# First attention of a fused block: the softmax weights scaled inside their transpose by a diagonal from VectorE, in place of a scaling on GpSimd

## What is computed

```python
# NSA half: 8 heads, two branches each that matter here (selected, window)
p = masked_softmax(q @ k.T * scale + bias, mask)      # [256 queries, 256 keys], causal
out = gate_c * o_c + gate_s * (p_s @ v_s) + gate_w * (p_w @ v_w)
# DSA half: 8 heads over a latent, keys chosen by an index score (top 64 of 256)
p = masked_softmax(q_lat @ c.T * scale + bias, chosen & causal)
o_lat = p @ c ;  o = o_lat @ w_uv
y = concatenate([out, o]) @ ev_w_out
```

## Time and profile before

| | |
|---|---|
| median of 3 runs | 1220.17 us (1218.13 to 1221.36) |
| the profiled execution | 1217.92 us, its span 1216.1 us |
| busy in the span | PE 1123.6 (92%), DVE 784.4 (64%), ACT 609.4 (50%), POOL 64.8 (5%) |
| chain that ended last | PE 75%, DVE 14%, ACT 6% |
| L1073, the scalings on POOL | 48 of them, 38.0 us busy, 805 ns mean |
| TensorE's granted clock, mean | 0.976 |

### The profile page before, as it was taken

How to read it: one execution, slowest core, us unless ns; L and a number is a source line. 1 busy time by engine, 2 the same in 40 slices (tenths; PEclk the granted TensorE clock), 3 DMA queues, 4 the chain that set the end, 5 groups by cost and what they waited for, 6 DMA issues and landing times.

```text
span 1216.1 us, 20615 instructions
## 1 busy us (share of the span) xinstructions
PE 1123.6 (92%) x8503; PEld 1004.0 (83%) x8503; DVE 784.4 (64%) x1288; ACT 609.4 (50%) x1097; POOL 64.8 (5%) x85
## 2 busy tenths in 40 slices
PE   1788999999999989989999999999789998999997
PEld 1766966889899889878899988998677887999996
DVE  7666684789898685557855446666766556444443
ACT  0341376554435356565454554546673436544543
POOL 0011086000000000000000000020000000000000
PEclk9999899999999999999999999989878999999999
DMA  8678712489999545423775653160000043655540
GB/s 369 260 291 316 270 47 70 137 297 361 361 340 347 198 150 181 173 75 130 281 259 189 227 174 107 70 237 6 1 2 20 2 153 113 211 200 176 200 144 35
DMA packets 33277, 218.31 MB, mean 180 GB/s; under 512 B 4496, under 2 KB 5264, under 8 KB 8480
## 3 DMA queue, kind: packets, MB, share of 16 engines
q1 hardware_dynamic: 33184, 217.00, 49.2%
HBM read 215.93 MB, written 1.05 MB: 178 GB/s over the span
## 4 chain that ended last, share of the span: by engine, by line
PE 75%; DVE 14%; ACT 6%; DMA 2%; issue 1%; POOL 0%; SPq 0%; DVEq 0%; ACTq 0%
PE bank L505 20%; PE bank L507 20%; PE bank L506 20%; DVE ada_acc L574 2%; PE bank L530 2%; DVE low L499 1%; DMA ring<-ada_halves 1%; DVE act_low L1450 1%; PE bank L2300 1%; PE bank L587 1%; PE bank L2302 1%; ACT high L493 1%; PE bank L1081 1%; PE bank L2288 1%; DVE y_tmp L1495 1%
## 5 line engine op out<-in xcount | busy, mean ns | idle before, releaser
L499 DVE TENSOR_TENSOR low<-ring,high 128x2048 fp32r<-128x2048 f32 (+1 forms) x139 | 317.8, 2288 | 256.2 <-ACT high L493 255.9
L493 ACT ACTIVATE high<-ring 128x2048 fp32r<-128x2048 f32 (+1 forms) x139 | 264.6, 1906 | 258.3 <-PE bank L507 199.3
L505 PE MATMUL bank<-act_high,high 128*128 128x256 f32 (+1 forms) x1112 | 321.1, 289 | 6.0 <-DVE act_low L1450 6.0
L507 PE MATMUL bank<-act_high,low 128*128 128x256 f32 (+1 forms) x1112 | 316.0, 284 | 0.0
L506 PE MATMUL bank<-act_low,high 128*128 128x256 f32 (+1 forms) x1112 | 315.7, 284 | 0.0
L505 PE MATMUL bank<-high,act_high 128*128 128x512 f32 (+1 forms) x632 | 233.8, 370 | 3.8 <-DVE act_low L2828 1.8
L506 PE MATMUL bank<-low,act_high 128*128 128x512 f32 (+1 forms) x632 | 231.4, 366 | 0.0
L507 PE MATMUL bank<-high,act_low 128*128 128x512 f32 (+1 forms) x632 | 231.3, 366 | 0.0
L505 PEld LDWEIGHTS bank<-act_high,high 128*128 128x128 f32 x1112 | 213.5, 192 | 11.2 <-DVE act_low L1450 6.8
L506 PEld LDWEIGHTS bank<-act_low,high 128*128 128x128 f32 x1112 | 213.5, 192 | 2.7 <-issue 1.7
L507 PEld LDWEIGHTS bank<-act_high,low 128*128 128x128 f32 x1112 | 213.3, 192 | 0.0
(11 more groups left out here) (479 smaller groups left out, 1325.6 us busy)
## 6 DMA issues: line engine op xcount, KB each, us to landing
ring<-chunks SPq DMA_DIRECT2D x138, 1024.0 KB, 5.0
ring<-ada_halves SPq DMA_DIRECT2D x48, 1024.0 KB, 5.6
ring<-raw_cmp SPq DMA_DIRECT2D x4, 1024.0 KB, 7.0
gate_rows<-ada_b SPq DMA_DIRECT2D x4, 512.0 KB, 6.6
bias<-bias_by_distance SPq DMA_DIRECT2D x1, 2048.0 KB, 11.8
ln_rows<-ln_g SPq DMA_DIRECT2D x4, 512.0 KB, 4.5
ln_rows<-ln_b SPq DMA_DIRECT2D x4, 512.0 KB, 6.0
hT<-xT SPq DMA_DIRECT2D x1, 1024.0 KB, 8.5
```

The source lines that it names most:

```text
L493: e.activation(weights(c)[0], in_ring(("w", c)), ACT.Copy).then_inc(*act.up("high", c))
L499: e.tensor_tensor(low, in_ring(("w", c)), high.bitcast(F32), ALU.subtract).then_inc(*vec.up("low", c))
L505: e.matmul(out_, ah, bh, start=start, stop=False)
L507: return e.matmul(out_, al, bh, start=False, stop=stop)
```

## The change

A row scaling commutes with the turn: the transpose of diag(c) z is z transposed times diag(c). The change drops step 5. In its place DVE writes, behind the coefficients of a unit, two 128x128 diagonals (the identity times the coefficients, one scalar per row; in the NSA half times the gate in the same instruction, so that the separate gate product L1329 goes). PE's turn multiplies `z` with the diagonals where it was multiplied with the identity; the shapes stay. The diagonals have three slots, at the place of a tile that the indexer is done with, and a slot is free when turn(u-3) is done, for which DVE now waits. POOL keeps `mask_bias` alone. No transfer is added, removed or moved.

```diff
@@ -389,6 +389,7 @@
         relu = mem.take("relu", 2, UC, at=ln_at + 2 * UC)
+        diag = mem.take("diag", 3, 2 * P, at=ln_at + 2 * UC)
@@ -1066,12 +1067,27 @@
-        def unit_scale_gpsimd(e, u):
-            z, st = z_of(u), st_of(u)
-            e.wait_ge(*vec.at("coef", u))
-            for t, c in PARTS:
-                x = e.tensor_scalar(z[:, c], z[:, c], st[:, 4 + t:5 + t], None, ALU.mult)
-                x.then_inc(*(pool.up("p", u) if t else pool.up()))
+        def unit_scale_vector(e, u, gate):
+
+            st = st_of(u)
+            if u >= 3:
+                e.wait_ge(*pe.at("turn", u - 3))
+            for t in range(QT):
+                c_, d_ = st[:, 4 + t:5 + t], diag[:, u % 3, tok(t)]
+                if gate is None:
+                    x = e.tensor_scalar(d_, ident, c_, None, ALU.mult)
+                else:
+                    x = e.tensor_scalar(d_, ident, c_, gate(t), ALU.mult, ALU.mult)
+                x.then_inc(*(vec.up("p", u) if t else vec.up()))
+
+        def scaled_turn_tensor(e, u):
+
+            z = z_of(u)
+            b = ps.take(e, ("turn", u), act, "pT", u)
+            e.wait_ge(*vec.at("p", u))
+            for i in range(3):
+                m = e.matmul(b[:, tok(i)], z[:, tok(i)], diag[:, u % 3, tok(min(i, 1))], start=True, stop=True)
+            m.then_inc(*pe.up("turn", u))
...
@@ -1183,7 +1199,7 @@
-                    unit_turn_tensor(e, 2 * d - 3, pool)
+                    scaled_turn_tensor(e, 2 * d - 3)
...
@@ -1320,14 +1336,13 @@
                 e.wait_ge(*act.at("e", u))
+                e.reciprocal(st[:, 4:6], st[:, 2:4]).then_inc(*vec.up("coef", u))
+                e.wait_ge(*vec.at("coef", u))
                 if u >= DSA0:
-                    e.reciprocal(st[:, 4:6], st[:, 2:4]).then_inc(*vec.up("coef", u))
-                    return
-                h, branch = NSA[u]
-                e.reciprocal(st[:, 4:6], st[:, 2:4]).then_inc(*vec.up("sums", u))
-                e.wait_ge(*vec.at("sums", u))
-                e.tensor_tensor(st[:, 4:6], st[:, 4:6], gates[:, :, 3 * h + 1 + branch], ALU.mult).then_inc(
-                    *vec.up("coef", u))
+                    unit_scale_vector(e, u, None)
+                else:
+                    h, branch = NSA[u]
+                    unit_scale_vector(e, u, lambda t: gates[:, t, 3 * h + 1 + branch:3 * h + 2 + branch])
@@ -1395,16 +1410,11 @@
-            for u in range(DSA0 + 8):
-                if u == 14:
-                    e.wait_ge(*vec.at("mask"))
-                    mask_bias(0)
-                    mask_bias(1)
-                h = u - DSA0 + 2
-                if 2 <= h < 8:
+            e.wait_ge(*vec.at("mask"))
+            for h in range(8):
+                if h >= 2:
                     e.wait_ge(*vec.at("z", DSA0 + h - 2))
-                    mask_bias(h)
-                unit_scale_gpsimd(e, u)
+                mask_bias(h)
```

More of the change, by code:

```diff
@@ L1208, in attention_tensor @@
                 if d >= 1:
-                    unit_turn_tensor(e, 2 * d - 2, pool)
+                    scaled_turn_tensor(e, 2 * d - 2)
             e.wait_ge(*act.at("ql", 7))
             sparse_logits_tensor(e, 0)
-            unit_turn_tensor(e, 13, pool)
+            scaled_turn_tensor(e, 13)
             sparse_logits_tensor(e, 1)
@@ L1218, in attention_tensor @@
             for r in range(2):
-                unit_turn_tensor(e, 14 + r, pool)
+                scaled_turn_tensor(e, 14 + r)
             for step in range(2, 8 + 4):
@@ L1226, in attention_tensor @@
                 if 0 <= h < 8:
-                    unit_turn_tensor(e, DSA0 + h, pool)
+                    scaled_turn_tensor(e, DSA0 + h)
                 if step == 3:
```

## The result

The changed kernel takes 1225.11 us, the median of 10 runs (1220.23 to 1225.88). The kernel before takes 1218.99 on the same chip, also in 10 (1215.26 to 1223.12). The ratio is 1.0042 with a 95% interval of 1.0031 to 1.0054: slower by 0.42%, 3.8 to 6.6 us. The forecast was 1221.3 and no measurable change. The profiled execution took 1225.44 us, its span 1223.5, at a mean granted clock of 0.971.

What follows compares the result with a forecast made beforehand. TensorE, 92% busy, was taken as the bound, so a gain must end in one of its waits. Lateness 2.5 plus new wait 0.5 less gain 1.85 gave 1.15 us more: 1220.17 + 1.15 = 1221.3 us, range 1218.0 to 1224.0.

Steps and rivals of the forecast that it cites:

- The step that failed: TensorE's turn as a product with diagonals: same shapes and type as the transpose, so taken to cost nothing.
- PE's own row: NSA half: TensorE's own work not later, since it too waits at turns for banks that z(7) to z(13) empty.
- DVE's lateness: NSA half: added VectorE work makes z(12) 1.93 us late, z(15) 3.22, the first output product 2.5 (1.4 to 4.1).
- Price of a diagonal: VectorE, per 128-column product: 0.25 us with two scalars (0.20 to 0.32), 0.20 with one; an NSA unit costs 0.43 more.
- the 0.70 of free lateness: Before the first output product: head_out(2), which empties its PSUM bank, can come 0.70 us later without delaying it.
- The rival in which all this is hidden: NSA half: at 0.27 us per unit, 0.17 per diagonal, VectorE's added work is hidden; 1218.8 us, chance 0.2.
- The estimate of 0.13 us for a product: VectorE's diagonal product priced by the errata rule: 0.13 us each, 0.18 more per unit; the sum would end at 1218.8.
- The new wait: Ahead of the second output product: coefficient(17) needs the slot turn(14) frees, which delays low(9) and head_out(3); 0.5 us lost.
- The gain in the last steps: Last steps: TensorE's waits for GpSimd's scaling go; 0.47 + 0.47 + 0.6 + 0.3 = 1.85 us gained.
- the four waits: Last steps: TensorE waits four times for GpSimd's scalings, 1.9 us together; 0.47, 0.47, 0.6 and 0.3 to be gained.
- the rival with the swallowed gain: Last steps: ACT's copies and rounding set the pace once GpSimd is gone, so no gain; 1223.2 us, chance 0.08.
- The clock rival: NSA half: TensorE idles more, the granted clock falls to 1.2 GHz, 3.4 us added; 1224.7 us, chance 0.07.

## Why the prediction was wrong

**The step that failed** is one sentence: "PE's turn has the same shapes and type, so I take it at nothing." Shapes and type are the same, the operation is not. The runs put 3.22 us there beside the diagonals and 6.75 without them. With 5.13 in place of 1.15 the sum would have come to 1225.3 beside the 1225.11 measured. That this is so near is partly luck: the kernel before took 1218.99 in ten runs and not the 1220.17 from which the sum started, so the runs differ by 6.1 us. The rows to see it stood in the prediction's own groups: L1081, three transposes in the code, is `x3`; L1039, one product of 256 columns in the code, is `x2`. An fp32 product counts twice in a row, a transpose once. The sum had no term for it and no rival did.

A rule of the Trainium skill bears on this: FP8 and Floating Point Precision, section TensorE Precision Notes, says that true fp32 takes four passes through the array. The trace shows two instructions per block and twice the time of the transpose: PE goes on 0.67 us behind a turn of three products and 202.92 - 202.59 = 0.33 behind one of three transposes, so 0.22 and 0.11 per block.

**PE's own row.** The prediction let PE wait for DVE throughout: "PE's own row of work is not later". After the change PE is busy for all 42.85 us of the first stretch. It is later by its own work, 4.21 us, and DVE's lateness is hidden beneath: adding the diagonals to the products moves the first output product from 42.84 to 42.85.

The other terms can be read only where the failed one is taken out, in the run with transposes and diagonals (timeline of DVE, then of PE):

```profile
170.95 0.28 DVE L1058 CUSTOM_DVE_ANT_0 zb<-bank,bias 128x128 f32<-128x128 f32 x1
...
179.46 0.42 DVE L1112 TENSOR_TENSOR act_low<-bank,act_high 128x256 fp32r<-128x256 f32 x1
...
186.83 0.48 DVE L1078 TENSOR_SCALAR diag<-cols,ust 128x128 f32<-128x128 f32 x2 [2.71 <-PE bank L1089]
187.23 2.28 DVE L500 TENSOR_TENSOR low<-ring,high 128x2048 fp32r<-128x2048 f32 x1
...
179.86 0.43 PE L1190 MATMUL bank<-pT,v_sw 128*64 128x256 f32 x1 [0.71 <-ACT pT L1104]
...
199.60 0.60 PE L1040 MATMUL bank<-ckvT,qlatT 128*128 128x256 f32 x2
200.13 0.55 PE L1089 MATMUL bank<-cols,zb 128*128 128x128 f32 x3
...
202.59 0.49 PE L1089 MATMUL bank<-cols,zb 128*128 128x128 f32 x3
202.92 0.60 PE L1251 MATMUL bank<-pT,ckv 128*128 128x256 f32 x2
...
204.57 0.60 PE L1040 MATMUL bank<-ckvT,qlatT 128*128 128x256 f32 x2
205.48 0.55 PE L1089 MATMUL bank<-cols,zb 128*128 128x128 f32 x3 [0.32 <-ACT pT L1104]
```

- **Price of a diagonal: right.** In the changed kernel a pair of L1080 lasts 0.60 and one 0.34, so they start 0.26 us apart (0.25 forecast), and L1078 0.48 - 0.28 = 0.20 (0.20 forecast; a pair of L1078 is in the rows further down):

```profile
L1080 DVE TENSOR_SCALAR diag<-cols,ust,gates x32: 334/344/915, 144.5 to 185.3; 128x128 f32<-128x128 f32 x32
...
L1078 DVE TENSOR_SCALAR diag<-cols,ust x16: 274/284/784, 186.5 to 214.1; 128x128 f32<-128x128 f32 x16
...
167.01 0.60 DVE L1080 TENSOR_SCALAR diag<-cols,ust,gates 128x128 f32<-128x128 f32 x2
```

- **DVE's lateness: nearly right as far as z(12), right in its end by luck.** z(12) starts 170.95 - 139.26 = 31.69 us behind the first logits, before 171.93 - 142.00 = 29.93: 1.76 late, 1.93 forecast. From there two errors cover each other. head_out(2) is 40.20 - 37.45 = 2.75 late and not 3.22, for most part because the two mask products ahead of z(15) (L1378 and L1380 of the changed file) run without POOL beside them: z(15) starts 0.67 behind the first of them, 1.00 before. And the 0.70 of free lateness isn't there. The first output product is 41.40 - 38.64 = **2.76** late, 2.5 forecast, and still starts 0.78 us behind head_out(2)'s end, 0.77 before, so that bank did not hold it. PE waits 0.71 us ahead of it for ACT's copy `pT`, which stands on ACT behind exp(15) and with it behind DVE. The rival in which all this is hidden is out: the pair starts 0.26 apart and PE idles 2.68 us. The estimate of 0.13 us for a product, worked out from the errata rule of the Trainium skill (VectorE: DVE Perf Modes, section on the TRN2 errata), agrees neither with the 0.20 nor with the 0.26 here.
- **The new wait: right.** low(9) at 187.23 stands behind the diagonals that waited 2.71 us for the turn. It costs 10.10 - 9.72 = 0.38, and with four slots the stretch is 0.43 shorter; 0.5 forecast.
- **The gain in the last steps: too large.** 24.52 - 23.29 = **1.23** us, 1.85 forecast; the in-place scaling on VectorE gives 1.22 by another way. The first waited turn moves from 0.91 behind the logits' second product to 200.13 - 199.60 = 0.53. The second stays at 205.48 - 204.57 = 0.91, and its row now names ACT's copy `pT`. This one of the four waits, forecast at 0.47, only changed its name; the rival with the swallowed gain was right in this place. The third and fourth bring 1.23 - 0.38 = 0.85 of 0.9. With no scaling at all the stretch takes 23.34, so nothing more was to be had.
- **Sum of these:** 2.76 + 0.38 - 1.23 = 1.91 us against 1.15. Without the failed term the time would have been 1220.17 + 1.91 = 1222.1, just above the forecast's own 1220.2 to 1222.0 and well inside the range.
- **The clock rival** named a time, 1224.7, near the measured one, by luck and a wrong mechanism: the clock is 1.00 in all three windows after, and PE idles less, not more.

Of what the prediction wanted to see, DVE was to have almost no idle time from 153 to 181. It has 28.00 - 25.95 = 2.05 us in 28, since PE now sets the pace. A turn in the last steps was to follow the last one by 2.4 us; it does so by 2.46 with transposes (202.59 - 200.13) and by 2.75 after.

low(9) begins 191.36 - 190.02 = 1.3 us behind the start of the row of turn(14) and turn(15), where 0.9 were forecast; the turn itself is longer:

```profile
190.96 0.48 DVE L1078 TENSOR_SCALAR diag<-cols,ust 128x128 f32<-128x128 f32 x2 [3.22 <-PE bank L1089]
191.36 2.28 DVE L500 TENSOR_TENSOR low<-ring,high 128x2048 fp32r<-128x2048 f32 x1
...
190.02 1.50 PE L1089 MATMUL bank<-diag,zb 128*128 128x128 f32 x12
```

DVE's wait of 3.22 us here costs nearly nothing: PE is busy for all but 0.08 us of the stretch.

**Where the change's time is**, in one line of attention lengths. The floor is 71.17. POOL's scaling adds 1.71 (before, 72.88). Diagonals with transposes would add 3.62. Products add 6.75, and the diagonals 0.09 on top (after, 78.01).

## What to carry to other kernels

Before a transpose on a nearly full TensorE becomes a product, count its instructions in rows of the same kernel: here an fp32 product is two per block and an fp32 transpose one, so a scaling "inside" the transpose is not free. Work that is moved to TensorE must be priced on TensorE even where shapes and types stay, because there 0.34 us per turn passed straight into the time. Idle time on the other engine is no shelter by itself: VectorE had 8 of 38.64 us to spare in the first stretch, and some 0.45 us more per unit (2 x 0.26 - 0.07) still cost 2.76, because PE waits for its results in turn. It cost 0.09 in all only once PE was full. And where two engines take turns as the limit, price a change with each half alone: here 3.62 and 6.75 gave 6.84 together.

## What the runs showed of the hardware that was not expected

A VectorE product with scalars takes much longer when it meets POOL's half of the mask bias: L1080 has 915 ns at most where its median is 344, and that one, at 181.88, lies beside two of POOL's additions. In the changed kernel, POOL and then DVE:

```profile
184.54 0.74 POOL L1410 TENSOR_TENSOR dbias<-bias,taken 128x256 f32<-128x256 f32 x1 [1.84 <-DVE ust L1339]
...
184.58 0.79 DVE L1080 TENSOR_SCALAR diag<-cols,ust,gates 128x128 f32<-128x128 f32 x1
```

POOL's addition runs from 184.54 to 185.28. The product that starts 0.04 us behind it takes 0.79 us instead of 0.34, to 185.37, 0.09 behind POOL's end. The Trainium skill says of this pair of engines (SBUF — State Buffer, section Who interferes with whom) that, where VectorE runs in a mode that uses two ports, the one that issues first holds the shared ports for the whole instruction and the other is fully blocked. The trace agrees for this product, which ends only when POOL has ended. It goes the other way too. Of the eight additions one took 2750 ns before (L1395), and none more than 836 after. It began 0.13 us behind low(9), which ran from 184.93 to 187.22:

```profile
185.06 2.75 POOL L1395 TENSOR_TENSOR dbias<-bias,taken 128x256 f32<-128x256 f32 x1
```

And the two mask products of 384 columns on DVE (L1378, L1380) took 359 and 361 ns after, where they took 538 and 509 while POOL was scaling.

That a whole run can go at about half TensorE's pace, with 537 ns for the median of a 256-column product instead of 283, came once in these runs; its repetition was normal. Its granted clock reads 1.00 from end to end, so this reading doesn't show it; the durations do. What brought it isn't known.
